# Two transformer blocks on one core: experts chosen by comparisons, and two changes of order in the mixers

## What is computed

```python
g = jax.nn.sigmoid(gates.reshape(bsz, s_len, N_BRANCH, D_MODEL) + b_gate)
ys = jnp.stack([y_a, y_b, y_c], axis=2)
merged = jnp.einsum('bsnk,nkd,bsnd->bsd', ys, w_branch, g)
return merged @ w_out
```

```python
scores = jax.nn.sigmoid((t @ router_w).astype(jnp.float32))
sel = scores + router_bias.astype(jnp.float32)
grp = sel.reshape(-1, N_GROUPS, E_PER_GROUP)
group_score = lax.top_k(grp, TOP_K)[0].sum(-1)
_, g_idx = lax.top_k(group_score, TOPK_GROUPS)
...
masked = jnp.where(expert_mask, sel, NEG_INF)
_, e_idx = lax.top_k(masked, TOP_K)
w = jnp.take_along_axis(scores, e_idx, axis=1)
w = w / jnp.sum(w, axis=-1, keepdims=True)
...
out = out + gates[:, e:e + 1] * (he @ w_down[e])
```

## Time and profile before

| | us |
|---|---|
| median of 3 runs | 2109.1 (2108.68 to 2111.03) |
| profiled execution | 2106.61 |
| its span, first to last instruction | 2104.8 |
| PE busy | 1967.4 (93%) |
| DVE busy | 1378.6 (65%) |
| ACT busy | 847.8 (40%) |

### The profile page before, as it was taken

One profiled execution on the slowest core, in us unless ns is written; L12 is line 12 of the kernel. 1 busy time (PEld: TensorE's weight loads), 2 busy tenths in 40 slices (PEclk: granted clock), 3 DMA queues, 4 the chain that ended last, 5 costly groups with the idle time before them and its releaser, 6 DMA issues.

```text
span 2104.8 us, 25824 instructions
## 1 busy us (share of the span) xinstructions
PE 1967.4 (93%) x9588; PEld 1437.4 (68%) x9588; DVE 1378.6 (65%) x2203; ACT 847.8 (40%) x1127; POOL 62.5 (3%) x95
## 2 busy tenths in 40 slices
PE   3899999998999999999999999998899989889998
PEld 2788777776888788778777888776544447764443
DVE  6889776767888788877776888876411146642112
ACT  3344554665443543454655534564200035421000
POOL 0000000000000000000000000021000001000000
PEclk9999999999999999999999999999899999989999
DMA  9999553435897789744444799763799996359997
GB/s 395 376 377 371 182 187 146 170 125 221 338 364 315 287 344 376 292 173 159 173 144 152 295 371 378 209 238 130 283 421 421 421 356 242 123 216 421 421 421 329
DMA packets 98192, 597.88 MB, mean 284 GB/s; under 512 B 20256, under 2 KB 23712, under 8 KB 27424
## 3 DMA queue, kind: packets, MB, share of 16 engines
q1 hardware_dynamic: 91616, 585.18, 71.1%
q10 hardware_dynamic: 6464, 11.15, 1.6%
HBM read 595.21 MB, written 1.09 MB: 283 GB/s over the span
## 4 chain that ended last, share of the span: by engine, by line
PE 72%; DVE 12%; DMA 7%; ACT 5%; issue 3%; POOL 1%; SPq 0%; DVEq 0%; ACTq 0%
PE gu L2718 11%; PE acc L2328 10%; PE acc L2332 10%; PE acc L2331 10%; PE tr L2718 7%; PE gu L2328 5%; DMA proj<-ada_stream 5%; PE gu L2332 5%; PE gu L2331 5%; DVE w_lo L1367 3%; PE acc L2718 3%; PE tr L2468 3%; ACT w_hi L701 2%; DVE tf L2182 2%; DVE proj L1432 2%
## 5 line engine op out<-in xcount | busy, mean ns | idle before, releaser
L1367 DVE TENSOR_TENSOR w_lo<-stage,w_hi 128x2048 fp32r<-128x2048 f32 x231 | 527.6, 2288 | 87.8 <-ACT w_hi L701 87.4
L701 ACT ACTIVATE w_hi<-stage 128x2048 fp32r<-128x2048 f32 x232 | 442.5, 1912 | 211.6 <-PE acc L2332 203.2
L1432 DVE SCALAR_TENSOR_TENSOR proj<-proj,c_row 128x1024 f32<-128x1024 f32 x240 | 291.6, 1218 | 51.3 <-DMA proj<-ada_stream 40.3
L2328 PE MATMUL acc<-w_hi,hT_hi 128*128 128x512 f32 x672 | 277.4, 413 | 6.8 <-DVE z_mix L2077 2.8
L2332 PE MATMUL acc<-w_hi,hT_lo 128*128 128x512 f32 x672 | 264.7, 394 | 0.0
L2331 PE MATMUL acc<-w_lo,hT_hi 128*128 128x512 f32 x672 | 264.2, 393 | 0.0
L2328 PE MATMUL gu<-w_hi,hT_hi 128*128 128x512 f32 x640 | 254.2, 397 | 8.3 <-DVE pair L1504 7.1
L2332 PE MATMUL gu<-w_hi,hT_lo 128*128 128x512 f32 x640 | 250.4, 391 | 0.0
L2331 PE MATMUL gu<-w_lo,hT_hi 128*128 128x512 f32 x640 | 250.0, 391 | 0.0
L2328 PE MATMUL acc<-w_hi,yT_hi 128*128 128x512 f32 (+1 forms) x460 | 180.8, 393 | 2.8 <-ACT proj L1147 2.7
L2332 PE MATMUL acc<-w_hi,yT_lo 128*128 128x512 f32 (+1 forms) x460 | 178.8, 389 | 0.0
(11 more groups left out here) (270 smaller groups left out, 2525.9 us busy)
## 6 DMA issues: line engine op xcount, KB each, us to landing
stage<-wstream SPq DMA_DIRECT2D x312, 1024.0 KB, 5.8
proj<-ada_stream SPq DMA_DIRECT2D x120, 1024.0 KB, 7.6
w_raw<-wstream SPq DMA_DIRECT2D x72, 1024.0 KB, 18.9
z_mix<-wstream SPq DMA_DIRECT2D x12, 1024.0 KB, 16.5
more_yT<-wstream SPq DMA_DIRECT2D x12, 1024.0 KB, 17.7
more_prob<-wstream SPq DMA_DIRECT2D x12, 1024.0 KB, 16.8
more_proj<-wstream SPq DMA_DIRECT2D x12, 1024.0 KB, 18.1
tok<-gate_rows SPq DMA_DIRECT2D x10, 512.0 KB, 4.3
```

What stands on the lines that cost most here:

```text
L701: act.activation(w_hi[:, n % PARTS, :], stage[:, n % STAGES, :], ACT.Copy).then_inc(hi_ready, 1)
L1367: dve.tensor_tensor(w_lo[:, n % PARTS, :], stage[:, n % STAGES, :], w_hi[:, n % PARTS, :].bitcast(F32), ALU.subtract).then_inc(chunk_ready, 1)
L1432: ins = dve.scalar_tensor_tensor(w, w, 1.0, c_row[:], ALU.mult, ALU.mult, accum_out=dst)
L2328: ins = pe.matmul(dst, l_hi, r_hi, start=start, stop=False, skip_group_check=True)
```

## The change

- *Choice.* Each score is compared with the four of its group: differences of all pairs (128 numbers for the two tokens of a partition), a comparison with a table `ties` (0, or the smallest normal number below 0 where the other has the lower index), and a count of those that beat it. Fewer than 1.5 means one of the best two; their sum is the group's score, and the groups are compared in the same way. The instruction that makes `sent` signals itself.
- *Placement.* It uses bank `acc[2]`, waits for three of the eight copies instead of all, has four matmuls instead of five, and the wait for all eight comes behind it. Slots count from 1, so no 1 is subtracted from the ranks.
- *Gather.* The first gather starts on a new signal `pick_half` after the first 128 tokens' selection and goes through the tokens in the outer loop.
- *Mixer, slot 19.* The block of the first tokens is taken ahead of the low part of the chunk.
- *Mixer, end.* The fill for the second tokens of the last half is returned to the caller. The first two turns wait for two sums only and stand ahead of it; `high_rows` waits for both fills ahead of the second tokens; the wait for all four sums stands ahead of the last two turns.

```diff
-                  ("rank", NT * EXP), ("grank", NT * GROUPS)):
+                  ("ties", GROUPS * GROUPS)):
...
+                    if q == 0 and t == 0:
+                        ins.then_inc(pick_half, 1)
                 ins.then_inc(pick_ready, 1)
...
+                    early = mine and MIX_FILL[s_] == ("B", 0, 1)
+                    if early:
+                        take_block(s_, 0)
                     if s_ < SLOT_HEADS - 1:
                         lo(n0 + MIX_PRE + s_ + 2)
...
-                    if mine:
+                    if mine and not early:
                         take_block(s_, 0)
...
+                    def beaten_by(out, v, d):
+
+                        n = v.shape[1] // 4
+                        rows = v.rearrange("p (g e) -> p g e", e=4)
+                        d4 = d.rearrange("p (g e f) -> p g e f", e=4, f=4)
+                        own(dve.tensor_tensor(d4, rows.unsqueeze(2).to_broadcast([P, n, 4, 4]),
+                                              rows.unsqueeze(3).to_broadcast([P, n, 4, 4]), ALU.subtract))
+                        d3 = d.rearrange("p (g x) -> p g x", x=16)
+                        own(dve.tensor_tensor(d3, d3, ties.to_broadcast([P, n, 16]), ALU.is_gt))
+                        own(dve.tensor_reduce(out, d.rearrange("p (a f) -> p a f", f=4), AX, ALU.add))
+
+                    beaten_by(beaten, sel, duel)
+                    own(dve.scalar_tensor_tensor(top, beaten, 1.5, sel, ALU.is_lt, ALU.mult))
+                    own(dve.tensor_reduce(best, top.rearrange("p (g e) -> p g e", e=4), AX, ALU.add))
+                    beaten_by(g_beaten, best, g_duel)
+                    own(dve.tensor_scalar(g_open, g_beaten, 0.5, None, ALU.is_lt))
+                    dve.scalar_tensor_tensor(sent.rearrange("p (g e) -> p g e", e=4),
+                                             beaten.rearrange("p (g e) -> p g e", e=4), 1.5, over(g_open, 4),
+                                             ALU.is_lt, ALU.mult).then_inc(sent_ready, 1)
...
-                    own(dve.scalar_tensor_tensor(rank_f, acc[:, 0, 0:R], 1.0, oh1, ALU.add, ALU.mult))
-                    own(dve.tensor_scalar(rank_f, rank_f, -1.0, None, ALU.add))
+                    own(dve.scalar_tensor_tensor(rank_f, acc[:, 2, 0:R], 1.0, sent, ALU.add, ALU.mult))
...
                 for t in range(NT):
+                    if t:
+                        for half in range(2):
+                            pe.wait_ge(fill_out[half], filled)
...
-                        pe.wait_ge(pick_ready, l * QUADS + q + 1)
+                        pe.wait_ge(pick_half, l + 1) if q == 0 else pe.wait_ge(pick_ready, l * QUADS + q + 1)
...
+                            if q == r == a == 0 and j == 2:
+                                pe.wait_ge(pick_ready, l * QUADS + 1)
...
-                    for t in range(NT):
+                    for t in range(NT if s_ < len(MIX_FILL) - 1 else 1):
                         fill(s_, t)
+                return lambda: fill(len(MIX_FILL) - 1, 1)
...
-                    pe.wait_ge(mg_ready, b["mg"])
+                    pe.wait_ge(mg_ready, b["mg"] - 2)
                     for r in range(2):
                         turn(b["u"] + r, merged(r))
+                    last_fill()
...
                     low_rows(b["n"], of(0))
+                    pe.wait_ge(mg_ready, b["mg"])
                     for r in range(2, 4):
...
-                    pe.wait_ge(h_ready, 8 * step[1] + 8)
-                    pe.wait_ge(sent_ready, step[1] + 1)
-                    bank, sent, before = acc[:, 0, :], rt[:, 3, :], cst("before")
+                    pe.wait_ge(h_ready, 8 * step[1] + 3)
+                    pe.wait_ge(sent_ready, step[1] + 1)
+                    bank, sent = acc[:, 2, :], rt[:, 3, :]
                     s0, s1 = sent[:, 0:EXP], sent[:, EXP:2 * EXP]
...
+                    small_mm(bank[:, 2 * EXP:3 * EXP], ones, s0, True, False)
+                    small_mm(bank[:, 2 * EXP:3 * EXP], ones, s1, False, True)
+                    small_mm(bank[:, 0:2 * EXP], cst("before"), sent, True, False)
+                    small_mm(bank[:, EXP:2 * EXP], ones, s0, False, True).then_inc(placed, 1)
                     pe.wait_ge(h_ready, 8 * step[1] + 8)
```

More of the change, by code:

```diff
@@ L2260, in _ @@
                     R = NT * EXP
-                    sc, sel, key, oh1, oh2, cmp_ = (rt[:, i, 0:R] for i in (0, 1, 2, 3, 4, 5))
-                    small = rt[:, 6, :]
-                    pairs = rt[:, 7, :]
+                    sc, sel, beaten, sent, g_duel, top = (rt[:, i, 0:R] for i in (0, 1, 2, 3, 4, 5))
+                    duel = rt[:, 4:8, :].rearrange("p a c -> p (a c)")
+                    best, g_beaten, g_open, total = (rt[:, 6, at:at + 8] for at in (0, 8, 16, 24))
+                    total = total[:, 0:NT]
+                    ties = cst("ties").unsqueeze(1)
                     def by_t(v, w=EXP):
@@ L2306, in _ @@
-                    own(dve.scalar_tensor_tensor(cmp_, oh1, -3 * BIG, cmp_, ALU.mult, ALU.add))
-                    first_of_max(cmp_, cst("rank"), EXP, oh2, small[:, 16:18])
-                    own(dve.tensor_tensor(oh1, oh1, oh2, ALU.add))
-                    dve.nop().then_inc(sent_ready, 1)
-                    own(dve.tensor_tensor(sc, sc, oh1, ALU.mult))
-                    own(dve.tensor_reduce(small[:, 16:18], by_t(sc), AX, ALU.add))
-                    own(dve.reciprocal(small[:, 16:18], small[:, 16:18]))
@@ L2313, in _ @@
-                    own(dve.tensor_tensor(gates[:], by_t(sc), over(small[:, 16:18], EXP), ALU.mult))
+                    def beaten_by(out, v, d):
[7 more added lines that the diff above has]
+                        own(dve.tensor_reduce(out, d.rearrange("p (a f) -> p a f", f=4), AX, ALU.add))
@@ L2315, in _ @@
+                    dve.wait_ge(sent_ready, step[1] + 1)
+                    own(dve.tensor_tensor(sc, sc, sent, ALU.mult))
+                    own(dve.tensor_reduce(total, by_t(sc), AX, ALU.add))
+                    own(dve.reciprocal(total, total))
+                    own(dve.tensor_tensor(gates[:], by_t(sc), over(total, EXP), ALU.mult))
                     dve.wait_ge(placed, step[1] + 1)
                     rank_f = rank[:].rearrange("p t e -> p (t e)")
-                    own(dve.tensor_reduce(fullest[:], acc[:, 0, R:R + EXP], AX, ALU.max))
+                    own(dve.tensor_reduce(fullest[:], acc[:, 2, R:R + EXP], AX, ALU.max))
@@ L2549, in gather @@
                         c = slice((2 * r + a) * P, (2 * r + a + 1) * P)
-                        for j, (h, t) in enumerate((h, t) for h in (h_hi, h_lo) for t in range(NT)):
+                        for j, (t, h) in enumerate((t, h) for t in range(NT) for h in (h_hi, h_lo)):
+                            if q == r == a == 0 and j == 2:
+                                pe.wait_ge(pick_ready, l * QUADS + 1)
                             ins = small_mm(dst[:, a], h[:, t, c], pick[:, q % 2, t].rearrange("p e s -> p (e s)"),
@@ L3210, in _ @@
                 elif kind == "mixer":
[L3211 removed]
+                    last_fill = mixer(b, step[1])
                 elif kind == "backT":
[L3213 removed]
+                    pe.wait_ge(mg_ready, b["mg"] - 2)
                     for r in range(2):
                         turn(b["u"] + r, merged(r))
+                    last_fill()
                 elif kind == "out":
@@ L3284, in constants @@
     put("before", (r[:, None] < r[None, :]))
-    put("slots", np.tile(r, (P, 1)))
+    put("slots", np.tile(r + 1, (P, 1)))
     keep = r[None, :] <= r[:, None]
@@ L3294, in constants @@
             put(f"{f}_{name}", fn(ang).astype(np.float32).reshape(NT, P, rot // 2).transpose(1, 0, 2))
-    put("rank", np.tile(np.arange(EXP, 0, -1), (P, NT)))
-    put("grank", np.tile(np.arange(GROUPS, 0, -1), (P, NT)))
+    g = np.arange(GROUPS)
+    put("ties", np.tile(np.where(g[None, :] < g[:, None], -np.finfo(np.float32).tiny, 0.0).reshape(1, -1), (P, 1)))
     return c
```

14 lines of the change are left out of this document (4 added, 10 removed).

## The result

The median is 2097.1 us (2095.0 to 2099.9, four runs) against 2110.1 for the kernel before beside it: ratio 0.9944, 95% interval 0.9926 to 0.9962. That is 13.0 us or 0.6%, clear of the scatter of the runs. The predicted time was 2097. Run again beside other kernels it gave 0.9934 (0.9912 to 0.9956). The profiled execution took 2099.1 with a span of 2097.3.

The account below looks back on a forecast made before the run. PE's own work was taken to bound most of the kernel, so an edit gains PE's idle time. Terms -2.8 (early block), -3.1 (mixer end), -4.8 (choice and gather start), -1.1 (clock) sum to -11.8: 2109.1 becomes 2097 us, range 2091 to 2105.

Parts of the forecast that it names:

- Early block: Slot 19 of each mixer: gate product ahead of the split removes PE's wait for its bank, -1.38 us per mixer.
- ACT's chain: Rival: ACT's rounding and exponentials set the pace of slots 20 to 23, PE waits there instead; 2100 us, chance 0.13.
- End of the mixer: Last fill of each mixer: first turns go ahead of it, low rows start 1.54 us earlier despite a new 0.7 wait.
- Choice: Expert routing, both layers: ten DVE instructions instead of 24 and a shorter placement, 2.4 us gained per layer.
- Start of the gather: Both expert layers: the branch, not the selection, holds the gather, which moves with the count by 2.4 us; -4.8 for both.
- the sign named: Sign of a right forecast: the gather starts 1.3 to 1.5 us after the count.
- The rival of the half signal: The branch is short and PE waits for the selection: another 0.8 us gained per layer; 2095.5 us, chance 0.12.
- Clock in the gather: The 32 gather matmuls of each layer: a clock drop is less likely, both taken at 5.59 us, -1.1 together.
- Passed on in full: Expert layers: an earlier gather moves both PE and the expert-weight stream, so the whole gain is passed on.
- transposes at the lower level: Rival: PE's 32 routing transposes run at half speed, 3.7 us more, and both gathers are slow; 2107 us, chance 0.08.
- fetch behind the branch: Rival: code after PE's branch is loaded behind queued weights, 21.7 us for one fetch; 2119 us, chance 0.02.

Follow-up runs that it names:

- the whole selection: After with the gather waiting for the complete selection, as before, without a signal on its first half: ratio 0.9941.
- the later counters: After with PE's two counter increments moved from between branch and gather to behind the gather's first round: ratio 0.9938.
- filled gap: After with three idle 128x512 matmuls put between the placement and PE's reading of the count: ratio 0.9931.

## Why the prediction was right, point by point

- **Early block**, taken at -1.38 for each mixer: -1.7. Mechanism right, ACT's chain did not take it back (no new wait of PE in slots 20 to 23, and none missing when the edit is undone). The term was too small because I took the listed idle time; the price runs from start to start.
- **End of the mixer**, -1.54: -1.2. All predicted waits are there, 1.51 and 0.25 gone, 0.7 new, and the split was what is late. The low part came about 0.1 later than reckoned, and behind the new pause PE restarts as slowly as behind the old. The errors of this term and the one before cancel, which is luck: 2.92 predicted for a mixer, 2.9 measured.
- **Choice**: right to the tenth. The string takes 1489.89 + 0.19 - 1487.59 = 2.49 (2.4 predicted), a wide instruction 0.29 (0.29), the placement follows the transposes directly and takes 1.04 (1.05). From the first sum or subtraction to the gather it was 1497.37 - 1489.25 = 8.12 and is 1493.28 - 1487.59 = 5.69: 2.43 gained, 2.4 predicted; in layer 1 2.34.
- **Start of the gather**: right. PE's own string from the count over the branch holds it, not the selection; shown by the whole selection (no change) and the later counters (0.3 to 0.4 earlier). It came 1.55 and 1.46 after the count, where 1.3 to 1.5 was the sign named. The rival of the half signal falls.
- **Clock in the gather**, -1.1: 4.13 and 5.55 against 6.71 and 5.59, so -2.6. In repeated profiles each gather is fast or slow, 12 of 20 fast, and after itself had the first fast and the second slow in one profile and the reverse in the other; so one price for both could not be right in every run.
- **Passed on in full**: this step failed in layer 0. It took DMA as idle up to the first chunk at 1506, but the load of gate rows stands in between (asked for at 1497.94 in the trace of before). A fast gather's 1.4 us are lost in the start of the chunk stream, beside the gate rows; the layer gains 3.4 to 4.1 in either case, and 5.0 only once that load is moved. In layer 1 it held: 2.3 to 2.6 with a slow gather, 3.3 to 4.0 with a fast one.
- **Other rivals.** No transposes at the lower level: the 32 take 3.7 us in all 14 profiles, and in the ten of the new route without filled gap the gather starts 17.1 to 17.7 us into the stage, where it was 19.9 to 20.1. No fetch behind the branch either, by the same numbers. The Trainium skill (Runtime: NRT & Kernel Launch, Instruction fetch mechanics) tells of such a wait for a taken branch; no run here shows it: from the count to the first matmul it is 1.0 to 1.6 us in every profile, and never the 21.7 of that rival.

The sum by undisturbed stages: 2 x 2.9 + 3.8 + 2.4 to 4.0, that is 12.0 to 13.6, against 11.8 predicted and 13.0 and 14.2 between the medians of the two series. That the time came out at 2097 to a tenth is partly luck: the gain was 13.0 and not 11.8, but before stood at 2110.1 beside it and not at the 2109.1 from which the forecast started; gains missed in one term were made good in another, and the stages that nobody touched move by several us from run to run.

## What to carry to other kernels

Price a pause of a pipelined engine from the start of the instruction before it to the start of the second behind it, less what that stretch takes without the pause; the listed idle time was 0.3 us short both times here. Where a part ahead of a saturated stream becomes faster, ask what else is in the queue when the stream starts, since only the stream's own earlier start is a gain. And when the untouched stages of a kernel spread by nearly as much as the change is worth, judge the parts by the lengths of their stages, look at the next stage too before calling a part a gain of the kernel, and leave the total to many runs.

## What the runs showed of the hardware

- After gets the fall of the clock in a gather in one profile and not in the other; a 3.4 us stretch at 0.50 cost 1.4 to 1.6 us where PE was busy in it, and nothing where it came in the pause between two stages (mixer and next pass 263.7 and 193.8 with such a fall at 504 us, and without).
- Moving the small store of gate values ahead of four weight loads did not bring its landing nearer: 22.2 us from the store to the load that waits for it in after, 23.2 with the move, and those weights then came at 420 GB/s still at 16 to 20 us of the stage, where in after nothing moved any more.
- Two empty counter instructions of PE between a branch and its first matmul cost 0.3 to 0.4 us.
